# A diffusion backbone's front: the shift job on TensorE from the weights, the scale job on VectorE, the loads in turn, the token copies shared

## The reference, cut to what matters

```python
def rms_norm(t, gain=None):
    y = (tf * lax.rsqrt(jnp.mean(tf * tf, axis=-1, keepdims=True) + EPS)).astype(t.dtype)
...
def modulate(t, shift, scale):
    return rms_norm(t) * (1 + scale) + shift
...
    sc = jax.nn.silu(c)
    scc = jax.nn.silu(c_ctx)
    h, hc = x, ctx
    for l in range(DEPTH):
        m = (sc @ w_mod[l] + b_mod[l]).reshape(bsz, N_MOD, 1, D_MODEL)
        mc = (scc @ w_mod[l] + b_mod[l]).reshape(N_MOD, D_MODEL)
        h = h + 0.5 * m[:, 2] * swiglu(modulate(h, m[:, 0], m[:, 1]), w_ff1_in[l], w_ff1_out[l])
        hc = hc + 0.5 * mc[2] * swiglu(modulate(hc, mc[0], mc[1]), w_ff1_in[l], w_ff1_out[l])
```

## Time and profile before

| | |
|---|---|
| median of three executions | 3232.58 us (3232.05 to 3235.33) |
| the profiled execution | 3239.35 us |
| its span, first to last instruction | 3237.5 us |
| TensorE's mean granted clock, share of full | 0.981 |
| TensorE busy | 3084.7 us (95%) |
| VectorE, ScalarE, GpSimd busy | 1932.5, 1138.7, 267.5 us |

### The profile page before, as it was taken

One profiled execution on the slowest core, in us unless ns is written; L12 is line 12 of the kernel. 1 busy time (PEld: TensorE's weight loads), 2 busy tenths in 40 slices (PEclk: granted clock), 3 DMA queues, 4 the chain that ended last, 5 costly groups with the idle time before them and its releaser, 6 DMA issues.

```text
span 3237.5 us, 43569 instructions
## 1 busy us (share of the span) xinstructions
PE 3084.7 (95%) x17705; PEld 2734.2 (84%) x17705; DVE 1932.5 (60%) x2657; ACT 1138.7 (35%) x1750; POOL 267.5 (8%) x319
## 2 busy tenths in 40 slices
PE   5999999998999998899999999999999999999999
PEld 4999999987669895488999988999998876678887
DVE  7754536535442636757778765877778568643333
ACT  5211212466441321235323334532223547542222
POOL 1100000200001005620000001000000100000000
PEclk8999999999999999999999999999999999999999
DMA  5533424322004220012343321333333120023332
GB/s 205 171 109 104 124 73 139 105 66 57 1 1 137 59 66 7 1 40 88 95 130 104 117 66 59 111 98 103 112 117 105 53 78 1 14 85 98 97 98 91
DMA packets 314303, 274.19 MB, mean 85 GB/s; under 512 B 17426, under 2 KB 290057, under 8 KB 313865
## 3 DMA queue, kind: packets, MB, share of 16 engines
q1 hardware_dynamic: 286992, 182.35, 18.9%
q0 software_dynamic: 25488, 89.14, 8.8%
q10 hardware_dynamic: 1641, 0.14, 0.0%
HBM read 263.21 MB, written 8.39 MB: 84 GB/s over the span
## 4 chain that ended last, share of the span: by engine, by line
PE 52%; DVE 3%; ACT 2%; issue 1%; POOL 0%; ACTq 0%; DVEq 0%
PE ps L2232 30%; PE ps L491 16%; PE ps L1449 1%; ACT gpt L1488 1%; DVE hs_lo L2425 1%; ACT gp L1501 1%; PE ps L1473 1%; PE ps L1431 1%; PE ps L1195 1%; PE ps L2314 0%; DVE vw_lo L2165 0%; PE ps L1887 0%; DVE ms_s L2456 0%; DVE h_sb L2433 0%; PE ps L1904 0%
## 5 line engine op out<-in xcount | busy, mean ns | idle before, releaser
L481 DVE TENSOR_TENSOR w_lo<-ring,w_hi 128x1024 fp32r<-128x1024 f32 (+3 forms) x221 | 252.3, 1143 | 470.8 <-ACT w_hi L466 382.1
L491 PE MATMUL ps<-u_hi,w_hi 128*128 128x384 f32 (+2 forms) x1584 | 466.5, 354 | 19.5 <-DVE u_lo L652 18.0
L491 PE MATMUL ps<-u_hi,w_lo 128*128 128x384 f32 (+2 forms) x1584 | 461.5, 351 | 0.0
L491 PE MATMUL ps<-u_lo,w_hi 128*128 128x384 f32 (+2 forms) x1584 | 461.3, 351 | 0.0
L466 ACT CAST w_hi<-ring 128x1024 fp32r<-128x1024 f32 (+3 forms) x157 | 149.3, 952 | 587.2 <-PE ps L491 554.6
L491 PEld LDWEIGHTS ps<-u_hi,w_hi 128*128 128x128 f32 x1584 | 285.0, 189 | 45.5 <-issue 22.3
L491 PEld LDWEIGHTS ps<-u_lo,w_hi 128*128 128x128 f32 x1584 | 285.4, 189 | 22.0 <-issue 1.4
L491 PEld LDWEIGHTS ps<-u_hi,w_lo 128*128 128x128 f32 x1584 | 284.9, 189 | 20.9
L2159 ACT CAST vw_hi<-ring 128x1024 fp32r<-128x1024 f32 (+1 forms) x176 | 181.2, 1031 | 343.0 <-PE ps L2232 285.0
L2165 DVE TENSOR_TENSOR vw_lo<-ring,vw_hi 128x1024 fp32r<-128x1024 f32 (+1 forms) x176 | 211.0, 1200 | 152.1 <-ACT vw_hi L2159 151.8
L2232 PE MATMUL ps<-u_hi,vw_hi 128*128 128x384 f32 x768 | 248.7, 338 | 12.9 <-DVE u_lo L652 12.3
(11 more groups left out here) (351 smaller groups left out, 5862.5 us busy)
## 6 DMA issues: line engine op xcount, KB each, us to landing
ring<-in_w_ff_in SPq DMA_DIRECT2D x176, 512.0 KB, 3.9
ring<-in_w_ff_out SPq DMA_DIRECT2D x72, 512.0 KB, 4.0
cst<-in_w_mod POOLq DMA_DIRECT2D x72, 512.0 KB, 3.9
m_in<-in_w_mod POOLq DMA_DIRECT2D x56, 512.0 KB, 4.0
ring<-in_w_in_e SPq DMA_DIRECT2D x26, 512.0 KB, 3.9
m_first<-in_w_mod POOLq DMA_DIRECT2D x16, 512.0 KB, 13.9
ring<-in_w_out_e SPq DMA_DIRECT2D x16, 512.0 KB, 3.8
ring<-in_w_ff_out SPq DMA_DIRECT2D x16, 384.0 KB, 3.3
```

The lines of the kernel that those rows point to most:

```text
L481: dve.tensor_tensor(w_lo[:, b:b + WIDE[n]], ring[:, s:s + WIDE[n]], w_hi[:, b:b + WIDE[n]], ALU.subtract).then_inc(w_split_lo, 1)
L491: mm = pe.matmul(ps_at(p, c0, c1) if halved else pair(p)[:, c0:c1], w, x[:, c0:c1], start=start and i == 0, stop=stop and i == 2)
```

## The change

The 16 pieces are now sent in turn, one of the scale, one of the shift, into twelve places of `m_first`, with six under way at most. VectorE makes the scale job alone, from the even pieces, as before. The shift job no longer passes VectorE: `pe_mod_through` multiplies each odd piece on TensorE, as the stationary operand, with two columns of activations, and adds up in PSUM over the eight pieces. SP waits for the twelfth piece ahead of the first ring chunk. ScalarE copies only the first two transposed blocks to `h`, VectorE the other six. TensorE's list has a new order, and the row-scale matmuls are two instead of six, over the same 768 columns.

```diff
-        m_first = at("m_first", 20 * T, 8 * D)
+        m_first = at("m_first", 16 * T, FIRST * D)
...
             for n in range(n_first):
-                if n >= 8:
-                    pool.wait_ge(m_used, n - 7)
-                pool.dma_start(m_first[:, D * (n % 8):D * (n % 8) + D],
-                               mod_src(JOBS[n // DB], n % DB)).then_inc(m_came[n % 8], 16)
+                if n >= 6:
+                    pool.wait_ge(m_came[n % 6], 16 * (n // 6))
+                if n >= FIRST:
+                    pool.wait_ge(m_through if n % 2 else m_used, (n - FIRST) // 2 + 1)
+                pool.dma_start(first_piece(n), mod_src(JOBS[n % 2], n // 2)).then_inc(m_came[n % 6], 16)
...
+        def pe_mod_through(pe, k):
+
+            n = 2 * k + 1
+            if k == 0:
+                pe.wait_ge(sc_done, 1)
+            pe.wait_ge(m_came[n % 6], 16 * (n // 6 + 1))
+            q = JOBS[1][1]
+            for d in range(DB):
+                c0 = 16 * q + 2 * d
+                mm = pe.matmul(bank(5, c0, c0 + 2), first_piece(n)[:, P * d:P * d + P], sc[:, 2 * k:2 * k + 2],
+                               start=k + d == 0, stop=k == DB - 1 and d == DB - 1)
+            mm.then_inc(m_mm if k == DB - 1 else m_through, 1)
...
+            sp.wait_ge(m_came[(FIRST - 1) % 6], 32)
             sync_ff(f, 0)
...
             pe.wait_ge(const_in, 16)
+            for k in range(4):
+                pe_mod_through(pe, k)
+            pe.wait_ge(rows_in, 16 * 24)
+            for n, rn in ((0, VA_N), (1, VB_N), (2, VC_N)):
+                mm = pe.transpose(bank(6)[:, P * n:P * n + rn], rows[0:rn, n, :], ident[0:rn, 0:rn])
+            mm.then_inc(vec_t, 1)
             pe.wait_ge(x_in, 16 * NT)
...
+                if d in (3, 4, 5):
+                    pe_mod_through(pe, d + 1)
+                if d == 5:
+                    pe_mod(pe, JOBS[0], 0, DB)
+            pe_mod_through(pe, 7)
             pe_norm_first(pe)
-            pe_mod_halves(pe, JOBS[1], 1, (5, 2))
-            pe.wait_ge(vec_done, 3)
             pe_ff(pe, 0)
...
-            for job in range(2):
-                dve_mod_first(dve, job)
-            dve.wait_ge(m_used, 2 * DB)
-            dve_fold(dve, JOBS[1], 1)
+            dve_mod_first(dve)
+            for d in range(2, DB):
+                dve.wait_ge(xt_done, d + 1)
+                dve.tensor_copy(h[:, d, :], pair(d % 2)).then_inc(h_loaded, 1)
```

More of the change, by code:

```diff
@@ L157, in at @@
             return nc.alloc_sbuf_tensor_at(name, [P, cols], dt, offset=arena + 4 * first)
+        FIRST = 12
         u_sb = at("u_sb", 0, 8 * T)
@@ L281, in build @@
         vec_t, vec_done, sc_done = sem("vec_t"), sem("vec_done"), sem("sc_done")
-        xt_done, h_loaded = sem("xt_done"), sem("h_loaded")
+        xt_done, h_loaded, h_act = sem("xt_done"), sem("h_loaded"), sem("h_act")
         c_in = sem("c_in")
         m_full = [sem("m_full0"), sem("m_full1")]
-        m_came = [sem(f"m_came{i}") for i in range(8)]
+        m_came = [sem(f"m_came{i}") for i in range(6)]
+        m_through = sem("m_through")
         m_used, m_fold, m_mm, mod_raw, mod_done = sem("m_used"), sem("m_fold"), sem("m_mm"), sem("mod_raw"), sem("mod_done")
@@ L517, in h_ready @@
             if n == 0:
-                eng.wait_ge(h_loaded, d + 1)
+                if d < 2:
+                    eng.wait_ge(h_act, d + 1)
+                else:
+                    eng.wait_ge(h_loaded, d - 1)
             else:
@@ L563, in pe_norm_first @@
             pe.wait_ge(r_act, 3)
-            for n in range(NT):
-                mm = pe.matmul(pair(3)[:, P * n:P * n + P], ones, rsn[:, P * n:P * n + P], start=True, stop=True)
+            pe.wait_ge(vec_done, 3)
+            for c0, c1 in ((0, 512), (512, T)):
+                mm = pe.matmul(pair(3)[:, c0:c1], ones, rsn[:, c0:c1], start=True, stop=True)
             mm.then_inc(n_rs, 1)
@@ L659, in pool_mod_first, with first_piece @@
             for n in range(n_first):
-                if n >= 8:
-                    pool.wait_ge(m_used, n - 7)
-                pool.dma_start(m_first[:, D * (n % 8):D * (n % 8) + D],
-                               mod_src(JOBS[n // DB], n % DB)).then_inc(m_came[n % 8], 16)
+                if n >= 6:
[3 more added lines that the diff above has]
+                pool.dma_start(first_piece(n), mod_src(JOBS[n % 2], n // 2)).then_inc(m_came[n % 6], 16)
+        def first_piece(n):
+            return m_first[:, D * (n % FIRST):D * (n % FIRST) + D]
+        def pe_mod_through(pe, k):
[9 more added lines that the diff above has]
+            mm.then_inc(m_mm if k == DB - 1 else m_through, 1)
         def pool_keep(pool):
@@ L694, in m_add, with dve_mod_first @@
             x.then_inc(m_used, 1)
-        def dve_mod_first(dve, job):
+        def dve_mod_first(dve):
             for k in range(DB):
-                n = DB * job + k
-                if n == 0:
+                n = 2 * k
+                if k == 0:
                     dve.wait_ge(sc_done, 1)
[L701 to L704, removed]
+                else:
+                    dve.wait_ge(m_used, k)
+                dve.wait_ge(m_came[n % 6], 16 * (n // 6 + 1))
+                m_add(dve, first_piece(n), k, 0)
         def dve_mod_piece(dve, n, x, k, slot_, first, jobs):
@@ L712, in dve_mod_piece @@
             m_add(dve, m_in[:, D * (n % 2):D * (n % 2) + D], k, slot_)
-        HALVED = [JOBS[1]] + [x for key in sorted(MODS) for x in MODS[key]]
+        HALVED = [x for key in sorted(MODS) for x in MODS[key]]
         HALF_BANKS = ((4, 7), (5, 6), (4, 7))
@@ L767, in dve_mod @@
                                              op0=ALU.add, op1=ALU.add)
+                if x == JOBS[1] and s == 0:
+                    y.then_inc(m_used, DB)
             y.then_inc(mod_raw, 1)
@@ L2689, in _ @@
             pe.wait_ge(const_in, 16)
+            for k in range(4):
[4 more added lines that the diff above has]
+            mm.then_inc(vec_t, 1)
             pe.wait_ge(x_in, 16 * NT)
             for d in range(DB):
-                if d >= 2:
-                    pe.wait_ge(h_loaded, d - 1)
+                if 2 <= d < 4:
+                    pe.wait_ge(h_act, d - 1)
+                elif d >= 4:
+                    pe.wait_ge(h_loaded, d - 3)
                 for n in range(NT):
@@ L2785, in _ @@
             act.preload_act_table_set(LN_EXP)
[L2786 to L2790, removed]
             act.wait_ge(vec_t, 1)
             for k, (v, rn) in enumerate(((va, VA_N), (vb, VB_N), (vc, VC_N))):
-                act.copy(v[:, :], bank(0)[:, P * k:P * k + rn]).then_inc(vec_done, 1)
+                act.copy(v[:, :], bank(6)[:, P * k:P * k + rn]).then_inc(vec_done, 1)
+            act.wait_ge(x_in, 16 * NT)
+            for d in range(2):
+                act.wait_ge(xt_done, d + 1)
+                act.copy(h[:, d, :], pair(d)).then_inc(h_act, 1)
+            act_norm_first(act)
             for c in range(2):
@@ L2840, in _ @@
                 dve_split(dve, BASE[NEXT[0]] + c)
-            dve_mod(dve, JOBS[1], 1, (5, 2))
+            dve_mod(dve, JOBS[1], 1)
             dve_norm(dve, 0)
```

## The result

The changed kernel takes 3255.73 us, the median of four runs (3252.8 to 3256.2), the kernel before 3233.95 beside it (four runs, 3232.05 to 3237.45). The comparison of the runs gives a ratio of 1.0055 with a 95% interval of 1.0043 to 1.0067: **slower by 0.55%**, some 18 us of 3232.58. The two medians are 21.8 us apart, a ratio of 1.0067, which is the upper end of that interval. The profiled execution of the changed kernel took 3252.80 us (span 3251.0), that of the kernel before 3239.35, so between the two traces there are 13.45 us to be found. Both traces have a mean granted clock of 0.981.

The account below looks back on a forecast made before the run. It took VectorE's chain to bound the front, then TensorE's tail: 35.5 us from a 39.3 release delays the first multiply 19.3, taken as 17 with a likely clock spell; 3232.58 + 17 gives 3249.5 us, range 3239 to 3255.

Parts of the forecast that it names:

- VectorE's gain: VectorE's multiply-adds on the first pieces, halved, end at 40.3 instead of 51.25: 11 us if VectorE still were last.
- Release by the small loads: TensorE's start on small rows and x waits for all 24 small loads, until 39.3 us (37.5 to 40.8).
- What stands behind it: On TensorE, 8.9 us of x transposes move from under the loads behind the 39.3 release, with passes, job and row scales.
- The tail on TensorE: TensorE's work from 39.3 through the row scales, 35.5 us at 1.2 GHz, ending at 74.8; first multiply 19.3 us later.
- the spell at 2.4 GHz: A short stretch of TensorE's tail at the higher clock, about as likely as not, worth 3 to 7 us.
- The way from trace to median: The front's whole shift reaches the end; 17 us added to the plain runs' median of 3232.58.
- What hides beside it: ScalarE's squares, scales (near 54) and ring splits, VectorE's six copies and the ring's loads stay covered by TensorE's tail.
- Rival one: TensorE's clock stays at 2.4 GHz through the tail: first multiply 5.0 us later, 3237.6 us, not slower; chance 0.10.
- Rival two: Small loads through before 31; TensorE then waits for VectorE's first copy at 41: 11.5 us later, 3244 us; chance 0.08.
- Rival three: Small loads early and clock up together: first multiply at 54.0, 1.5 us earlier than before, 3231 us; chance 0.05.
- Rival four: The split does nothing for the end: VectorE's 11 us fall on a chain no longer last; part of the forecast.

Follow-up runs that it names:

- e1: Changed kernel with TensorE's transposes of the small rows moved back behind the eight blocks of x, ahead of the last weight pass; 3251.88 us (before: 3234.52).
- e3: Changed kernel with five untransposed small loads on their own semaphore, so TensorE waits for the other 19 only; 3243.40 us (before: 3234.52).
- e6: Kernel before, with only SP waiting for the twelfth piece ahead of the first ring chunk; 3237.15 us against 3237.44.
- e2: Kernel before, with only the small rows and ScalarE's copies of them moved ahead of x; 3249.05 us (before: 3234.52).
- e4: As e3, but ScalarE copies all eight blocks of x, which stand together behind three passes, other passes and job following; 3241.53 us (before: 3234.52).
- e5: As e4, but passes hold the activation columns and stream 512 weight columns, last pass ahead of the scale job; 3233.47 us against 3237.44, ratio 0.9987.
- e7: Changed kernel in its own order, small rows still ahead of x, with the wide passes of e5; 3252.01 us (before: 3236.93).

## Why the prediction was right

The forecast was "slower", by a mechanism with an order of steps, and the steps are there one by one. The size is at the edge: the median of 3255.73 is 0.7 us above the range, while the ratio applied to 3232.58 gives 3250.4, 0.9 from the forecast of 3249.5. That nearness is in part luck, as the tail and the way to the median show below.

- *VectorE's gain.* Through at 40.3 forecast, 40.71 measured. This is closer than the sum was: 34 and 15 turns of 0.190 are 36.9 for the last piece, not 37.7, which would have given 39.4; the piece was awaited until 38.23. e1 and e3 show that this end still counts: their fifth block waits for it at 41.6 and 41.8.
- *Release by the small loads.* 39.3 forecast (37.5 to 40.8), 40.08 measured; of the 1.4 us that I took off for shorter turns 0.7 came. e6, which holds back the ring alone, got 40.90. The step that was wrong is that the end of the small loads follows the turns of the whole queue: the last 26 or 27 packets come at 5 to 8 a microsecond, with the ring held back or not.
- *What stands behind it.* e2 shows that the moved wait by itself costs 12.1 us at the first multiply, the size of the whole loss. But e1 and e3 show that it isn't the only cause: without it, VectorE's copies hold the fifth block, TensorE's passes and job follow, and the loss stays at 9 to 12 us. e4, where ScalarE copies all blocks and they stand together, takes 5.2 of e3's 9.2 us away, and e5's wide passes the other 4.0 and 4.7 more. The causes overlap, and so the costs may not be added.
- *The tail on TensorE.* 35.5 us at 1.2 GHz forecast, 28.0 measured (40.08 to 68.08). By start times: the blocks 8.4 for 10.2, the passes 9.05 for 14.1, the job 6.8 for 7.0, the rows and the scales as forecast. Nearly all of the difference is the spell at 2.4 GHz of 45 to 51.2, worth 6.9 us here with the overlap of neighbouring rows. I had given such a spell 3 to 7 us and counted 2.3 of it: this term was sized too small for this trace. A pass was 3.4 to 3.57 and 1.85 us, forecast 3.5 and 1.8.
- *The way from trace to median.* I took the shift in the front over to the median as it stands. The front of the profiled execution moved by 12.6 us and the execution by 13.45, the median by 21.8. So the front moved by less than the 17 us that I counted and the median by more, and the two misses offset each other in part. The profiled run of the changed kernel is the fastest of its four, that of the kernel before (3239.35) slower than the four others. The three slower runs of the changed kernel have a mean granted clock of 0.979 to 0.980, the profiled one 0.981. That the spell is shorter in them would fit, but no run shows their fronts; this stays open.
- *What hides beside it.* The row scales were ready at 53.24 (54 forecast), and the ring's split began at 53.15: neither is waited for.
- *Rival one* (2.4 GHz throughout) came in part: the clock rose with the transposes and stayed for two passes and part of the third, then fell with TensorE busy. Read as I had put it, the Trainium skill (TensorE: Matmul & The Clock Gate, Part 1) would have kept it up; the rows of 51.2 to 65 (0.50 at full occupation) differ, and the measurement decides. *Rival two* (small loads early) was made in e3: the fifth block waits for VectorE's copy until 41.83, 41 in the rival; the first multiply came at 64.71 for 67. *Rival three* as written (small loads early and the clock up throughout) wasn't made; e5, which also moves the blocks and widens the passes, gets ahead of the kernel before. *Rival four* holds: from 40.08 on, no row of TensorE in the changed kernel waits for VectorE, up to the layer's first matmul, so its 10.5 us (51.25 to 40.71) are gained where nothing ends.

## What to carry to other kernels

Before moving a wait forward on an engine, list what is queued behind it and ask what covered that work so far: here 8.9 us of transposes lay at no cost under the loads, and one wait for all of 24 small loads, five of them needed by nobody there, took the cover away. Taking work from the engine whose chain ends last gains only what the next chain leaves; count the receiving engine's new work at the level of clock that such work gets, and give a product with few columns the shape in which the wide operand streams. When a wait is removed and nothing is gained, look for the second one at the same time before giving up the theory.

## What the runs showed of the hardware that was not expected

- TensorE full of matmuls of one or two columns lost the higher clock: in e4 it fell near 38.2, in the middle of such passes, and stayed at 1.2 GHz for the 15 us to 53.1 and beyond; in e5 passes of 512 columns kept 2.4 for 8.6 us. The early passes, alone between waits for pieces, say the same: in the changed kernel all four took 3.55 to 3.57 us, at 1.2 GHz; in e7, in the same places, two of the four wide ones took 1.88.

```profile
27.04 1.88 PE L682 MATMUL ps<-m_first,sc 128*2 128x512 f32 x4 [1.72 <-DMA m_first<-in_w_mod]
```

- At the same level the two shapes cost the same: a pass of sixteen instructions on full weight tiles took 1.85 us at 2.4 GHz and 3.57 at 1.2, one of four instructions of 512 columns 1.75 to 1.88 and 3.57. On the passes themselves the wide shape gained through the clock alone.
- Holding back one of three queues brought the other two little, and not in every run: in 26 to 36 us the seven runs with the ring held back moved 837 to 973 packets of the pieces and 820 to 862 of the small loads, the two with it 879 and 771, 867 and 772. The small loads ended at 39.3 us (e5) to 41.95 (e2), in every trace behind a few last packets at 5 to 11 a microsecond.
